# A streaming encoder layer on eight cores: write-backs, rope tables, state transfers and the down projection's last blocks rearranged

## What is computed

```python
h = LN1(ALPHA * x + 0.5 * (silu(x @ wg1) * (x @ wu1)) @ wd1)     # hidden width 2816
z = h @ w_in                                  # q (512) | k, v (128 each) | x_lru | gate_lru (512 each)
A = windowed_attention(rope(q), rope(k), v)   # chunks of 64, own chunk and the 2 before it, sinks
B = rg_lru(conv4(x_lru)) * gelu(gate_lru)     # a scan over time
h = LN2(ALPHA * h + concat(A, B) @ w_out)
h = LN3(ALPHA * h + 0.5 * (silu(h @ wg2) * (h @ wu2)) @ wd2)
y = h + sigmoid(h @ w_ple_gate) * (p @ w_ple)
```

## Time and profile before

| | |
|---|---|
| three runs | 5180.85 us median (5179.34 to 6000.52) |
| profiled execution | 5182.85 us, 2.0 us above the median of the runs |
| its span, by core | 5152.4 to 5180.7 us; the page and the rows are of core 0, the longest |
| mean granted PE clock, by core | 0.975 (core 0) to 0.981 |
| busy | PE 94%, DVE 58%, ACT 33%, POOL 12% of the span |
| PE clock granted in the 40 slices | 9 tenths or more nearly throughout, 8 in the first two and 7 in the last but one |
| transfers | 956.25 MB; share of the 16 engines 0.9 in the first two slices, mostly 0.5 to 0.7 later |

### The profile page before, as it was taken

How to read it: one execution, slowest core, us unless ns; L and a number is a source line. 1 busy time by engine, 2 the same in 40 slices (tenths; PEclk the granted TensorE clock), 3 DMA queues, 4 the chain that set the end, 5 groups by cost and what they waited for, 6 DMA issues and landing times.

```text
span 5180.7 us, 80081 instructions; the slowest of 8 cores (5152.4 to 5180.7 us)
## 1 busy us (share of the span) xinstructions
PE 4867.6 (94%) x24230; PEld 2284.7 (44%) x24711; DVE 3015.1 (58%) x4850; ACT 1734.0 (33%) x3749; POOL 604.2 (12%) x1069
## 2 busy tenths in 40 slices
PE   6898798999989999999999999999999999999958
PEld 3344343444444444444444444444444444444423
DVE  3356555656565565666656566665656656565554
ACT  1053432515243152332515243251514334151421
POOL 1012111001010010101001010100101010110110
PEclk8899899999999999999999999999999999999979
DMA  9958967675745757566675756657575666857464
GB/s 210 209 155 191 205 218 152 177 221 157 213 131 159 228 159 214 172 192 189 171 227 157 214 171 198 195 165 218 159 220 169 200 186 174 216 152 218 152 123 147
DMA packets 506192, 956.25 MB, mean 185 GB/s; under 512 B 269328, under 2 KB 278096, under 8 KB 505776
## 3 DMA queue, kind: packets, MB, share of 16 engines
q1 hardware_dynamic: 242064, 828.92, 49.9%
q0 software_dynamic: 31392, 64.50, 8.4%
q10 hardware_dynamic: 232320, 57.70, 7.6%
HBM read 880.76 MB, written 77.09 MB: 185 GB/s over the span
## 4 chain that ended last, share of the span: by engine, by line
PE 70%; DVE 9%; DMA 7%; issue 7%; ACT 5%; POOL 1%; SPq 1%; ACTq 0%; DVEq 0%; POOLq 0%
PE ps_all L346 69%; DVE L_xc L389 2%; ACT P L372 2%; DMA pbuf<-p 1%; DMA bring<-wbg 1%; DVE lnst L574 1%; DMA actT<-nb 1%; DVE hbuf L389 1%; ACT Pb L372 1%; PE ps_all L350 1%; DMA rope_c<-rope 1%; DVE ft L389 1%; DMA wsb<-bring 1%; DVE tmp L919 1%; DVE hid L380 1%
## 5 line engine op out<-in xcount | busy, mean ns | idle before, releaser
L346 PE MATMUL ps_all<-actT,bring 128*128 128x512 bf16 x11020 | 2508.0, 382 | 80.3 <-DMA bring<-wbg 42.8
L346 PEld LDWEIGHTS ps_all<-actT,bring 128*128 128x128 bf16 x11264 | 1101.0, 98 | 1386.6 <-issue 133.6
L346 PE MATMUL ps_all<-bring,hid 128*128 128x512 bf16 x5493 | 1275.9, 382 | 41.3 <-DVE hbuf L389 16.1
L372 ACT ACTIVATE ft<-ps_all 128x512 f32<-128x512 f32 x748 | 427.5, 573 | 1937.6 <-PE ps_all L346 1803.2
L389 DVE SCALAR_TENSOR_TENSOR ft<-ft,ps_all 128x512 f32<-128x512 f32 x748 | 491.1, 657 | 631.4 <-ACT ft L372 563.0
L346 PEld LDWEIGHTS ps_all<-bring,hid 128*128 128x128 bf16 x5632 | 545.2, 98 | 670.6 <-issue 87.2
L389 DVE SCALAR_TENSOR_TENSOR hbuf<-hbuf,ps_all 128x512 f32<-128x512 f32 x384 | 249.7, 683 | 566.1 <-PE ps_all L346 565.5
L380 DVE TENSOR_TENSOR hid<-ft,ps_all 128x512 bf16<-128x512 f32 x704 | 479.8, 682 | 86.8 <-PE ps_all L346 62.6
L389 DVE SCALAR_TENSOR_TENSOR hbuf<-hbuf,lnst,gbuf 128x1024 f32<-128x1024 f32 x384 | 485.4, 1279 | 3.2 <-DVE hbuf L389 1.7
L346 PE MATMUL ps_all<-actT,fring 128*128 128x512 bf16 x1615 | 382.2, 380 | 10.3 <-ACT P L372 4.1
L394 ACT CAST nb<-hbuf 128x1024 bf16<-128x1024 f32 x192 | 199.1, 1042 | 277.7 <-DVE hbuf L389 165.8
(11 more groups left out here) (126 smaller groups left out, 3222.9 us busy)
## 6 DMA issues: line engine op xcount, KB each, us to landing
bring<-wsb SPq DMA_DIRECT2D x970, 512.0 KB, 4.1
fring<-wsf SPq DMA_DIRECT2D x255, 512.0 KB, 4.8
bring<-wbg POOLq DMA_DIRECT2D x64, 512.0 KB, 17.2
wsb<-bring SPq DMA_DIRECT2D x64, 512.0 KB, 9.8
hbuf<-x SPq DMA_DIRECT2D x64, 512.0 KB, 7.7
y<-hbuf SPq DMA_DIRECT2D x64, 512.0 KB, 5.6
gbuf<-ln_g SPq DMA_DIRECT2D x48, 512.0 KB, 5.9
gbuf<-ln_b SPq DMA_DIRECT2D x48, 512.0 KB, 6.6
```

Of the source, the lines that this page charges most:

```text
L346: return P.op("pe", lambda e: e.matmul(out, lhsT, rhs, start=start, stop=stop), reads, writes, cost=(max(0.056, fsz(rhs) * 0.00042), 0.165 ...
L372: return P.op("act", lambda e: e.activation(out, in_, func, **kw), reads, writes, cost=acost(out, func))
```

## The change

It has four parts. (1) A cast block's write-back is no longer issued together with the cast. It is kept in a list `pend` and issued by `write_back`: when the planner's clock has passed the estimated landing of the cast (called in each round of the planner), or before the slot or the block is used again. (2) The sine table gets a name of its own, `rope1`, and so doesn't wait for the cosines. (3) Both states live in one [128, 16] tile per kind (`hst`). The sample's states are loaded early in rows (`l0`) into `vfin`, transposed on PE and copied by ACT (`li`); at the end PE transposes the tile, ACT copies it into `vfin` and two transfers store rows of 128 elements (`hx`, which now waits for the step `vx` that stores the last values from the same buffer). (4) The last two dn blocks of each half (4 and 5) are worked through by token quarters: block 4 and then block 5 for quarter 0, both for quarter 1, and so on.

```diff
-    hcar = sb("hcar", [128, 4])
-    hcars = sb("hcars", [128, 4])
-    halo = sb("halo", [128, 4, 3])
-    halos = sb("halos", [128, 4, 3])
+    hst = [sb("hst%d" % i, [128, 16]) for i in range(2)]
+    vfin = sb("vfin", [128, 128])
+    halo, halos = [h[:, 0:12].rearrange("p (r c) -> p r c", r=3) for h in hst]
+    hcar, hcars = [h[:, 12:16] for h in hst]
...
                 nm = "%s%d" % (self.pre, i % n)
                 slot = self.slots[i % n]
+                self.write_back(nm)
                 if bi not in self.seen:
                     self.seen.add(bi)
                     dma("pool", slot[:, 0:w], self.src[bi][:, 0:w], (), (nm,), nm + "p")
-                    dma("sp", self.ws[bi][:, 0:w], slot[:, 0:w], (nm,), ("%sw%d" % (self.pre, bi),), nm + "w")
+                    self.pend.append((nm, bi, w, slot))
                 else:
+                    for q in [q for q in self.pend if q[1] == bi]:
+                        self.write_back(q[0])
                     dma("sp", slot[:, 0:w], self.ws[bi][:, 0:w], ("%sw%d" % (self.pre, bi),), (nm,), nm)
                 self.next += 1
+
+        def write_back(self, name=None, now=None):
+
+            for q in list(self.pend):
+                nm, bi, w, slot = q
+                if nm == name or (now is not None and P.last_w[nm].fin <= now):
+                    self.pend.remove(q)
+                    dma("sp", self.ws[bi][:, 0:w], slot[:, 0:w], (nm,), ("%sw%d" % (self.pre, bi),), nm + "w")
...
     for t, b in bg_seq:
-        ts_ = [t] + ([ride[(b[1], t)]] if (b[1], t) in ride else [])
-        for tt_ in ts_:
+        if b[0] == "dn" and NDN - 2 <= b[3] < NDN - 1:
+            continue
+        for tt_ in [t] + ([ride[(b[1], t)]] if (b[1], t) in ride else []):
...
+            half = b[4] if len(b) > 4 else None
+            for s in range(geom(tt_)[1]) if half is None else (2 * half, 2 * half + 1):
+                for b3 in [b[3]] if b[3] < NDN - 1 else range(NDN - 2, NDN):
+                    bg_steps.append(dn_step(b[1], tt_, b[2], b3, s, t, half))
...
             dma("sp", rope_c[:, 0:T], rope_d[0, :, pos0:pos0 + T], (), ("rope",), "rope")
-            dma("sp", rope_s[:, 0:T], rope_d[1, :, pos0:pos0 + T], (), ("rope",), "rope")
-        ini.append(Step(("rope", t), rope_load, (), ("rope",), (("k", mp),) if mp is not None else ()))
+            dma("sp", rope_s[:, 0:T], rope_d[1, :, pos0:pos0 + T], (), ("rope1",), "rope1")
+        ini.append(Step(("rope", t), rope_load, (), ("rope", "rope1"), (("k", mp),) if mp is not None else ()))
...
             def li():
-                for cc in range(4):
-                    dma("sp", halos[:, cc, :], sc_d[:, cc * 128:(cc + 1) * 128].rearrange("r p -> p r"),
-                        (), ("halos%d" % cc,), "car%d" % cc, nonc=True)
-                dma("sp", hcars[:], sh_d.rearrange("(c p) -> p c", p=128), (),
-                    ["hcs%d" % c for c in range(4)], "carh", nonc=True)
+                bk = take_bank()
+                tp(psum[bk][:, 0:16], vfin[0:16, :], ident[0:16, 0:16], ("vfin",) + CONST, ("ps%d" % bk,))
+                cp("act", hst[1][:], psum[bk][:, 0:16], ("ps%d" % bk,),
+                   ["halos%d" % c for c in range(4)] + ["hcs%d" % c for c in range(4)])
+
+            def l0():
+                dma("sp", vfin[0:12, :], sc_d.rearrange("r (c p) -> (r c) p", p=128), (), ("vfin",), "car")
+                dma("sp", vfin[12:16, :], sh_d.rearrange("(c p) -> c p", p=128), (), ("vfin",), "carh")
...
             def hx():
-                for cc in range(4):
-                    dma("sp", outs_state[tag]["c"][:, cc * 128:(cc + 1) * 128].rearrange("r p -> p r"),
-                        ha_[:, cc, :], (han % cc,), (), "st_c%d" % cc, nonc=True)
-                dma("sp", outs_state[tag]["h"].rearrange("(c p) -> p c", p=128), hc_[:],
-                    tuple(hcn % c for c in range(4)), (), "st_h", nonc=True)
-            lr.append(Step(("hx", t), hx, tuple(hcn % c for c in range(4))))
+                bk = take_bank()
+                tp(psum[bk][0:16, 0:128], hst[1 if sample else 0][:], ident[:],
+                   tuple(han % c for c in range(4)) + tuple(hcn % c for c in range(4)) + CONST, ("ps%d" % bk,))
+                cp("act", vfin[0:16, :], psum[bk][0:16, 0:128], ("ps%d" % bk,), ("vfin",))
+                dma("sp", outs_state[tag]["c"].rearrange("r (c p) -> (r c) p", p=128), vfin[0:12, :], ("vfin",), (), "st_c")
+                dma("sp", outs_state[tag]["h"].rearrange("(c p) -> c p", p=128), vfin[12:16, :], ("vfin",), (), "st_h")
+            lr.append(Step(("hx", t), hx, tuple(hcn % c for c in range(4)), (), (("vx", t),), nbank=1))
...
         now = P.free["pe"]
+        BR.write_back(now=now)
+        FR.write_back(now=now)
```

More of the change, by code:

```diff
@@ L761, in build @@
                     bg_steps.append(up_step(b[1], tt_, b[2], gu, t))
-            else:
-                for s in (range(geom(tt_)[1]) if len(b) == 4 else (2 * b[4], 2 * b[4] + 1)):
-                    bg_steps.append(dn_step(b[1], tt_, b[2], b[3], s, t, b[4] if len(b) > 4 else None))
+                continue
+            half = b[4] if len(b) > 4 else None
+            for s in range(geom(tt_)[1]) if half is None else (2 * half, 2 * half + 1):
+                for b3 in [b[3]] if b[3] < NDN - 1 else range(NDN - 2, NDN):
+                    bg_steps.append(dn_step(b[1], tt_, b[2], b3, s, t, half))
     streams = []
@@ L900, in mixer @@
         vpre = (("vi", t),) if t else ()
+        if sample:
+            vpre += (("li", t),)
         other = [m for m in mseq[:mseq.index(t)] if m >= NP - 1]
@@ L951, in fk @@
                    ("tmp0", "tmp1"), ("kfin",))
-        inp.append(Step(("k", t), fk, lambda: a_names(ak) + ("rope",), ("tmp0", "tmp1"), kpre, nbank=1, fgb=(kkey,)))
+        inp.append(Step(("k", t), fk, lambda: a_names(ak) + ("rope", "rope1"), ("tmp0", "tmp1"), kpre, nbank=1, fgb=(kkey,)))
         for s in range(nsub):
```

13 lines of the change are left out of this document (7 added, 6 removed).

## The result

| | before | after |
|---|---|---|
| median of runs | 5180.85 us | 5137.0 us (5133.47 to 5934.83, 5 runs) |
| ratio | | 0.9918, 95% interval 0.9899 to 0.9938 |
| profiled execution | 5182.85 us | 5141.17 us |
| spans by core | 5152.4 to 5180.7 | 5108.8 to 5139.6 |
| slowest core | 0 | 5 |

What follows compares the result with a forecast made beforehand. TensorE was taken as nearly full in the middle (81 us idle), with about 230 us idle at both ends. Terms 12 + 19 + 11 + 3 + 8 + 3 - 1 = 55 us off 5182.85 gave about 5128; 8-in-10 range 5096 to 5163.

Steps and rivals of the forecast that it cites:

- The 11 us of the middle: Down-projection tails, 900 to 4920 us: 11 of 14.9 us of TensorE's waits on bank evacuations go.
- the case that had 0.97: Whole kernel: time changes by no more than 2% either way, chance 0.97.
- Part 2: State writes at sample tile and end: transposing through TensorE removes slow stretches, gaining 12 and 19 us.
- the 12 of core 0's single wait: Sample tile: a 10.70 us weight wait and 1.6 us of half clock go, together 12 us.
- Part 1: Start and second cast phase: later write-backs and separate rope tables gain 3 and 8 us.
- The 8 us of the second cast phase: Second feed-forward weight casts, 446 to 616 us: TensorE's two waits shrink by 8 us, bounds 0 and 21.3.
- Part 3: Last two down-projection blocks by token quarters: 11 us from bank evacuations, 3 us from norm chains.
- The norms' term (3): Norms after down-projection, at both program ends: an earlier start gains 3 us, bounds 0 and 6.
- Another cause of the slow stretches: Rival, state writes: norm tables or any small write slow memory, so 31 us stay; 5159 us, 14%.
- the stall as bound: Rival, start: SP's wait behind the rope table is the bound, 27.6 us more go; 5100 us, 12%.
- the ring running short: Rival, 64 down-projection tails: late weight loads cost 1.8 us each, 115 us; 5243 us, 4%.
- Nothing moves on balance: Rival, middle and mixer's tail: the planner's new order eats what the waits give back; 5175 us, 8%.

Runs made afterwards that it cites:

- e7: The changed kernel without the new state handling, states stored by elements as before; ratio 0.9938 to the kernel before.
- e1: The kernel before with only the states transposed on TensorE and moved in rows; ratio 0.9963 to the kernel before.
- e15: Repeat of e1: the kernel before with only the states transposed and moved in rows; ratio 0.9943 to the kernel before.
- e3: The kernel before with only the later write-backs and the second rope table's own name; ratio 0.9970 to the kernel before.
- e4: The changed kernel without the token quarters in the last two down blocks; ratio 0.9937 to the kernel before.
- e12: The kernel before with only the second rope table's own name; ratio 0.9995 to the kernel before.

## Why the prediction was right or wrong

**The time** was right: 5137.0 against 5128, inside the range of its own case (5112 to 5145). Part of that is luck: 43 us came by the course where the sum had 55. The 11 us of the middle did not come at all (-1.3), and in the rest 7 us too few at the sample and 7.5 too many at the end stand against each other.

**The step that failed** is "A measurement of this kernel can tell some 2% (104 us) from no change". The chances stand on it. Taken by their letter, over 2% or not, the result lies in the case that had 0.97; but with them I said that the change can't be told from none, and it was told: the first comparison has an interval of 0.4% in all, and its half width is 10 us, not 104. By my own cases 5128 (60%), 5100 (12%) and 5159 (14%, 22 us below before) lie beyond that, so some 86% had to stand at a gain that can be told. Faster had 0.02. Two of the three runs of before, 5179.34 and 5180.85, showed how close executions lie; I had them in the table.

**In the sum**, the step that failed in its mechanism is "I take 11: a bank's evacuation, a DVE backlog of about 1 us aside, now has at least 1.3 us to itself": the runs show -1.3 us in the middle of after (0 to some 5 by all runs), since waits for ACT took the place of the waits for DVE. The other misses are mostly of size.

**Part 2** right in cause and about right in total (27 us by the course in e7, 19 and 30 alone by the ratios, against 30), wrong in the shares of its two places. At the sample, part 2 alone gains 15.6 and 14.6 us (e1, e15), 3 more than the 12 of core 0's single wait; the rest up to 19.4 are short waits of before (for `lruT` 3.5, `ft` 2.4, `pbuf` 2.4 us on core 0) which stay in e1 and go in the new order. At the end the term was sized on core 0 alone, and it was one of the cores that had it worst. Core 0 waited 22.91 us for the projection block, core 3 25.26, but the mean over the eight is 13.6 (1.5 in after), and core 5 of before waited only 7.22 there, and for a norm:

```profile
4978.58 1.01 PE L346 MATMUL ps_all<-fring,pT 128*128 128x512 bf16 x2 [7.22 <-DVE lnst L574]
```

so the mean gain is 11.5, not 19 and a share of the norms (9.1 and 9.3 with part 2 alone). The worst core's wait goes, and then another core is the slowest: core 0 gained 66 us, core 5 only 26. The landing under 8 us behind the store is met in the median (4.0 us on core 5) but not by every load: the longest takes 8.2 us on core 5 and 13.1 on core 7, and the waits at 800 and 4950 are 0 and 4 us. The Trainium skill's "DMA: Bandwidth & Descriptors", section "Specifications", has 512 bytes as the smallest transfer for full rate and says that below it the engines read, modify and write. The runs agree as far as they go: behind the 4-byte pieces 16 to 46 GB/s move, behind rows of 512 bytes 213 and 225. That the small pieces are slow by reading, modifying and writing no run here shows.

**Part 1** right for the start: share unchanged (0.96 and 1.03 at 206 to 209 GB/s), first statistics 5 us earlier, and 5.1 us at the end of the first up blocks with part 1 alone (the 22nd product of e3) against 3. The 8 us of the second cast phase it doesn't give alone. By the 88th product e3 is 4.0 us early and e4, parts 1 and 2, 5.4; only with the quarters is it 12.2 (e7) and 13.3 (after). From the 45th to the 66th product PE waits 41.9 us in e3 and 29.3 in after, in the mean over the cores, against 33.2 before. So the 13.3 against 11 is the work of parts 1 and 3 together, which the sum did not foresee. The Trainium skill's "DMA: Bandwidth & Descriptors", section "Issuing engines are not separate DMA queues", by which transfers from all issuing engines run on the same 16 engines and interleave, agrees with e12: SP's stall of 33 us gone, and 0.9995. The rule that a reordering of a full pipe gives back only its hole had one gap: fewer bytes in the same stage were to be had. In the second cast phase ACT still stands 13.9 us on one transposing transfer, and PE waits 15.48 us for a transfer of that kind at 613 us on core 5, the longest of the eight (7.3 in the mean); I had counted that wait as only partly curable.

**Part 3** right in the total alone (12 against 14), and that by luck, since it is wrong in the step named above. The waits on the evacuation fall from 14.9 to 2.3 us on core 5, more than forecast. But a wait that ends a microsecond before the next chain is ready isn't worth its length. My lower bound said it ("0 if another DVE operation is late instead"); it is ACT that is late, with 11.7 us for `LU`, and I chose close to the upper bound without having looked at what ACT had in hand at these 24 places. The norms' term (3) can't be found: behind the 683rd product, the first of the last feed-forward, PE stood idle 13.6 us before and 13.0 in after, in the mean over the cores.

**The rivals.** Another cause of the slow stretches, the stall as bound, and the ring running short are refuted (in the whole run of after PE waits 0 to 6.2 us a core for resident background blocks, 0.6 on core 5, where 64 tails would have cost 115; so my sign "if PE waits for resident weight blocks in the middle" was too sharp, since one core's single wait of 6.19 us at 1078 us meets it). "Nothing moves on balance" is true of the middle alone.

## What to carry to other kernels

Before a percentage is put on "no change", read from the runs how far two executions of one kernel lie apart, not from a round figure. Size a term on all cores: what the slowest core of one execution waits for is partly its own accident, and the program's time falls by what the next core allows. For a short wait that recurs at one place, ask what every other engine has in its queue at that moment, and count only the distance to the next one that would be late; in a stage that the transfers fill, count bytes, and look for bytes that a later, emptier stage can carry.

## What the runs showed of the hardware

Scattered 4-byte stores slow all transfers of a core, weight loads included: behind 512 of them core 2 moved nothing for 4.6 us, behind 1536 for 7.6, and with all 2048 on each of eight cores resident loads took up to 32.8 us where the usual is 4, at a share of 1.00 to 1.25 and 16 to 46 GB/s. A transposing transfer that ACT issues into full engines holds ACT for 13.9 us in after (core 5) and 15.62 before (core 0); the median over all such transfers is 1.2 us on either. The kernel before took 5180 us (median) in the first comparison and 5184 to 5201 in those on four other chips, the changed one 5137 and 5148 to 5152. That is up to 0.4%, as much as a part of this change is worth, so that only kernels run side by side can be compared; one chip alone gave 5189 and 5197 on two occasions.
